# A chunked scan inside a block kernel: the levels' decay factors as products, and one product per head and level

## The reference

```python
f = lbh + (1.0 - lbh) * sig              # forget factor in (0,1), sig = sigmoid(f_pre)
k = (1.0 - lbh) * (1.0 - sig)
# hgrn2_chunk_scan: S_t = diag(f_t) S_{t-1} + k_t v_t^T,   o_t = S_t^T q_t
```

## Time and profile before

| | us |
|---|---|
| median of three runs | 2431.41 (2431.05 to 2433.28) |
| profiled execution | 2433.08 |
| its span | 2431.2 |
| granted clock of TensorE, share of full | 0.992 |
| PE busy | 2378.2 |
| DVE busy | 1647.9 |
| ACT busy | 1178.0 |
| POOL busy | 46.9 |

### The profile page before, as it was taken

One profiled execution on the slowest core, in us unless ns is written; L12 is line 12 of the kernel. 1 busy time (PEld: TensorE's weight loads), 2 busy tenths in 40 slices (PEclk: granted clock), 3 DMA queues, 4 the chain that ended last, 5 costly groups with the idle time before them and its releaser, 6 DMA issues.

```text
span 2431.2 us, 30510 instructions
## 1 busy us (share of the span) xinstructions
PE 2378.2 (98%) x11924; PEld 2020.3 (83%) x11924; DVE 1647.9 (68%) x2155; ACT 1178.0 (48%) x1483; POOL 46.9 (2%) x36
## 2 busy tenths in 40 slices
PE   8999999999999999997999999999999999999998
PEld 8989787888888888886888888887888888888886
DVE  5884756777676676676666777555767567765775
ACT  5443545544544544545555443445655345544554
POOL 0330000000000000000000000000000000000000
PEclk9999999999999999998999999999999999999999
DMA  7434555887888888874988887554555655555554
GB/s 246 139 130 163 175 200 196 296 285 281 285 288 284 274 290 288 276 271 175 338 288 296 285 278 258 185 196 158 189 186 188 194 189 190 186 194 191 186 186 149
DMA packets 152492, 550.06 MB, mean 226 GB/s; under 512 B 17952, under 2 KB 19232, under 8 KB 151456
## 3 DMA queue, kind: packets, MB, share of 16 engines
q1 hardware_dynamic: 152352, 548.12, 66.3%
HBM read 545.94 MB, written 2.11 MB: 225 GB/s over the span
## 4 chain that ended last, share of the span: by engine, by line
PE 92%; DVE 4%; ACT 2%; issue 1%; DMA 1%; SPq 0%; POOL 0%; DVEq 0%; ACTq 0%
PE bank L426 20%; PE bank L428 20%; PE bank L427 20%; PE bank L409 7%; PE mis L409 7%; PE bank L413 3%; PE mis L413 3%; PE bank L397 2%; PE bank L398 2%; PE bank L399 2%; PE mis L427 1%; PE mis L426 1%; PE mis L428 1%; PE mis L518 1%; DVE wlo L1134 1%; PE mis L500 1%
## 5 line engine op out<-in xcount | busy, mean ns | idle before, releaser
L1134 DVE TENSOR_TENSOR wlo<-raw,whi 128x1024 fp32r<-128x1024 f32 x824 | 1005.3, 1225 | 698.9 <-ACT whi L724 698.3
L724 ACT ACTIVATE whi<-raw 128x1024 fp32r<-128x1024 f32 x824 | 868.2, 1059 | 1075.6 <-PE bank L428 650.9
L426 PE MATMUL bank<-whi,xs 128*128 128x512 f32 x1152 | 456.0, 396 | 4.8 <-DVE wlo L1134 3.1
L428 PE MATMUL bank<-wlo,xs 128*128 128x512 f32 x1152 | 450.6, 391 | 0.0
L427 PE MATMUL bank<-whi,xs 128*128 128x512 f32 x1152 | 450.2, 391 | 0.0
L426 PE MATMUL bank<-whi,hs 128*128 128x512 f32 x1072 | 417.9, 390 | 1.3 <-DVE wlo L1134 1.3
L428 PE MATMUL bank<-wlo,hs 128*128 128x512 f32 x1072 | 417.3, 389 | 0.0
L427 PE MATMUL bank<-whi,hs 128*128 128x512 f32 x1072 | 417.2, 389 | 0.0
L426 PEld LDWEIGHTS bank<-whi,xs 128*128 128x128 f32 x1152 | 217.4, 189 | 50.3 <-issue 6.7
L428 PEld LDWEIGHTS bank<-wlo,xs 128*128 128x128 f32 x1152 | 217.3, 189 | 46.1
L427 PEld LDWEIGHTS bank<-whi,xs 128*128 128x128 f32 x1152 | 217.5, 189 | 43.7
(11 more groups left out here) (189 smaller groups left out, 2058.2 us busy)
## 6 DMA issues: line engine op xcount, KB each, us to landing
raw<-wstream SPq DMA_DIRECT2D x824, 512.0 KB, 4.3
aring<-astream SPq DMA_DIRECT2D x192, 512.0 KB, 5.0
x<-xt SPq DMA_DIRECT2D x4, 512.0 KB, 6.6
gvb<-gvrow SPq DMA_DIRECT2D x8, 256.0 KB, 5.6
gate<-gate_rows SPq DMA_DIRECT2D x2, 1024.0 KB, 9.2
out<-acc SPq DMA_DIRECT2D x2, 640.0 KB, 3.6
pw<-poolw SPq DMA_DIRECT2D x1, 1024.0 KB, 10.5
silu_c<-rows SPq DMA_DIRECT2D x1, 1024.0 KB, 5.5
```

Of the source, the lines that this page charges most:

```text
L426: pe.matmul(o, h, whi[:, slot, c], start=first and k == 0, stop=False)
L428: mm = pe.matmul(o, h, wlo[:, slot, c], start=False, stop=last and k == UK - 1)
L724: act.activation(whi[:, slot, :], raw[:, slot, :], ACT.Copy).then_inc(hi_ready, 1)
L1134: dve.tensor_tensor(wlo[:, slot, :], raw[:, slot, :], whi[:, slot, :].bitcast(F32), ALU.subtract).then_inc(lo_ready, 1)
```

## The change

The levels run from small to large (`LEVELS` is now 1, 2, ..., 128) and no logarithm or exponential is taken. An item is the diagonal (`it` = 0) or a level (`it` = 1 to 8); PE does item `it` behind unit `it` + 4 of the half.

- `prep` writes the keys of the second tile of 128 tokens in reversed order. The first query operand is `qq` times the forget factor.
- `grow(hf, it)` on DVE comes ahead of the split at unit `it` + 4. It waits for the products of level `it`, multiplies neighbouring block products of forget factors to those of the next level (`spans`), and multiplies the keys of the left blocks and the queries of the right blocks in place.
- `both(hf, it)` on ACT copies the live half of the keys of each tile into one operand `kc`. Since the second tile is reversed, its left blocks fall where the first tile has right blocks, so both fit in 128 columns.
- `level` then has one product of 128 columns a head: the queries of the right blocks of both tiles, read in place from `qe` with gaps. Half of the result is of no use (keys of one tile with queries of the other), and `keep` takes the rest with two masked copies of 256, one a tile.
- `turn` reverses the second tile's `vv` over its tokens by a product with the reversed unit matrix, so that they fit the reversed rows of `sc`; ACT copies them back. `weigh` moves from behind unit (6,1) to behind (6,3), ACT's copy of its result from (6,3) to (6,5).
- POOL's program goes, and the fills of `kl` and `ones128` at the start. A second mask is loaded, and `eye_back` is made in `bounds`.

```diff
-LEVELS = (128, 64, 32, 16, 8, 4, 2, 1)
+LEVELS = (1, 2, 4, 8, 16, 32, 64, 128)
+ITEMS = 1 + len(LEVELS)
+ITEM_AT = 4
...
+        def item(hf, it):
+            return hf * ITEMS + it
+        def same_bank_before(hf, it):
+            if it >= 3:
+                return item(hf, it - 2)
+            return item(0, ITEMS - 3 + it) if hf else None
+        def span_at(l):
+            return 4 * T - 2 * (4 * T // LEVELS[l])
...
-            def level(hf, l):
-                i = l % 2
-                b = mis[i]
-                pe.wait_ge(h_ops, hf * 8 + l + 1)
-                if two_before(hf, l) is not None:
-                    pe.wait_ge(h_evac, two_before(hf, l) + 1)
-                if LEVELS[l] == 128:
+            def level(hf, it):
+                m, b = LEVELS[it - 1], mis[it % 2]
+                pe.wait_ge(h_ops, hf * len(LEVELS) + it)
+                if same_bank_before(hf, it) is not None:
+                    pe.wait_ge(h_evac, same_bank_before(hf, it) + 1)
+                if m == P:
                     for h in range(4):
-                        mm = pe.matmul(b[:, h * P:(h + 1) * P], kl[:, i, h * T:h * T + P],
-                                       qe[:, i, h * P:(h + 1) * P], start=True, stop=True)
+                        mm = pe.matmul(b[:, h * P:(h + 1) * P], kk[:, h * T:h * T + P], qe[:, h * T + P:(h + 1) * T],
+                                       start=True, stop=True)
                 else:
-                    for s in range(8):
-                        h, tt = s // 2, s % 2
-                        mm = pe.matmul(b[:, s * 64:(s + 1) * 64],
-                                       kl[:, i, h * T + tt * P:h * T + (tt + 1) * P],
-                                       qe[:, i, s * 64:(s + 1) * 64], start=True, stop=True)
+                    pe.wait_ge(h_both, hf * (len(LEVELS) - 1) + it)
+                    for h in range(4):
+                        k = slice(h * P, (h + 1) * P)
+                        mm = pe.matmul(b[:, k].rearrange("p (n m) -> p n m", m=m), kc[:, it % 2, k],
+                                       halves(qe[:, h * T:(h + 1) * T], m)[:, :, 1, :], start=True, stop=True)
                 mm.then_inc(h_sc, 1)
 
             def diagonal(hf):
-                pe.wait_ge(lg_sum, hf + 1)
+                pe.wait_ge(h_keys, hf + 1)
                 if hf:
-                    pe.wait_ge(h_evac, half_level(0, len(LEVELS)) + 1)
+                    pe.wait_ge(h_evac, 1)
                 for s in range(8):
                     h, tt = s // 2, s % 2
                     mm = pe.matmul(mis[2 + tt][:, h * P:(h + 1) * P], kk[:, h * T + tt * P:h * T + (tt + 1) * P],
                                    qq[:, 4 * hf + h, tt * P:(tt + 1) * P], start=True, stop=True)
                 mm.then_inc(h_sc, 1)
 
+            def turn():
+                pe.wait_ge(h_evac, 2 * ITEMS)
+                pe.wait_ge(bank_free, 12)
+                for c in range(2):
+                    mm = pe.matmul(mis[c][:, :], eye_back[:, :], vv[:, 1, c * NC:(c + 1) * NC], start=True, stop=True)
+                mm.then_inc(h_turn, 1)
             def weigh():
-                pe.wait_ge(h_evac, half_level(1, len(LEVELS)) + 1)
-                pe.wait_ge(bank_free, 12)
+                pe.wait_ge(h_turned, 2)
                 for hh in range(HEADS):
                     hf, h = hh // 4, hh % 4
                     c = slice(h * P, (h + 1) * P)
...
-            for l in range(9):
-                work[(2 + (l + 5) // 8, (l + 5) % 8)] = (0, l)
-                work[(4 + (l + 5) // 8, (l + 5) % 8)] = (1, l)
+            for hf, j0 in ((0, 2), (1, 4)):
+                for it in range(ITEMS):
+                    work[(j0 + (it + ITEM_AT) // GU, (it + ITEM_AT) % GU)] = (hf, it)
...
-                        hf, l = work[(j, u)]
-                        level(hf, l) if l < len(LEVELS) else diagonal(hf)
+                        hf, it = work[(j, u)]
+                        level(hf, it) if it else diagonal(hf)
                     if (j, u) == (6, 1):
+                        turn()
+                    if (j, u) == (6, 3):
...
+            def both(hf, it):
+                m = LEVELS[it - 1]
+                act.wait_ge(h_ops, hf * len(LEVELS) + it)
+                if it >= 3:
+                    act.wait_ge(h_sc, item(hf, it - 2) + 1)
+                o = halves(kc[:, it % 2, :], m).rearrange("p (h n) s m -> p h n s m", h=4)
+                k = halves(kk[:, :], m).rearrange("p (h a n) s m -> p h a n s m", h=4, a=2)
+                for a in range(2):
+                    ins = act.activation(o[:, :, :, a, :], k[:, :, a, :, a, :], ACT.Copy)
+                ins.then_inc(h_both, 1)
...
+                    if (j, i) in ((2, 0), (4, 0)):
+                        prep(j // 2 - 1)
...
+                        it = (j - j0) * GU + i - ITEM_AT + 1
+                        if 1 <= it < len(LEVELS):
+                            both(hf, it)
+                    if (j, i) == (6, 1):
+                        act.wait_ge(h_turn, 1)
+                        for c in range(2):
+                            act.activation(vv[:, 1, c * NC:(c + 1) * NC], mis[c][:, :], ACT.Copy).then_inc(h_turned, 1)
+                    if (j, i) == (6, 5):
...
             def prep(hf):
                 dve.wait_ge(h_sg, hf + 1)
...
+                    dve.wait_ge(h_sc, ITEMS)
+                k, g = (a[:, :].rearrange("p (h t) -> p h t", h=4) for a in (kk, sgf))
+                dve.tensor_scalar(k[:, :, 0:P], g[:, :, 0:P], -1.0, 1.0, ALU.mult, ALU.add)
+                link(dve.tensor_scalar(k[:, :, P:T], g[:, :, T - 1:P - 1:-1], -1.0, 1.0, ALU.mult, ALU.add))
+                for h in range(4):
+                    hh, c = 4 * hf + h, slice(h * T, (h + 1) * T)
+                    ins = dve.tensor_scalar(kk[:, c], kk[:, c], oml[:, hh:hh + 1], None, ALU.mult)
+                ins.then_inc(h_keys, 1)
                 for h in range(4):
                     hh, c = 4 * hf + h, slice(h * T, (h + 1) * T)
                     ins = dve.tensor_scalar(fft[:, c], sgf[:, c], oml[:, hh:hh + 1], lbt[:, hh:hh + 1], ALU.mult, ALU.add)
                 ins.then_inc(h_ff, 1)
...
+                dve.wait_ge(h_ff, hf + 1)
...
+                dve.tensor_tensor(qe[:, :], qh, fft[:, :], ALU.mult).then_inc(h_ops, 1)
+            def grow(hf, it):
+                l, m = it - 1, LEVELS[it - 1]
+                n = 4 * T // (2 * m)
+                of = fft[:, :] if l == 0 else spans[:, span_at(l):span_at(l) + 2 * n]
+                of = of.rearrange("p (n s o) -> p n s o", s=2, o=1)
+                dve.wait_ge(h_sc, item(hf, it) + 1)
+                dve.wait_ge(h_ops, hf * len(LEVELS) + it)
+                q = halves(qe[:, :], m)[:, :, 1, :]
+                if m < P // 2:
+                    o = spans[:, span_at(it):span_at(it) + n].rearrange("p (n o) -> p n o", o=1)
+                    dve.tensor_tensor(o, of[:, :, 0, :], of[:, :, 1, :], ALU.mult)
+                f = of.rearrange("p (h a n) s o -> p h a n s o", h=4, a=2)
+                for a in range(2):
+                    k = halves(kk[:, :], m).rearrange("p (h a n) s m -> p h a n s m", h=4, a=2)[:, :, a, :, a, :]
+                    fk = f[:, :, 1, ::-1, 1, :] if a else f[:, :, 0, :, 1, :]
+                    dve.tensor_tensor(k, k, fk.to_broadcast([P, 4, n // 8, m]), ALU.mult)
+                dve.tensor_tensor(q, q, of[:, :, 0, :].to_broadcast([P, n, m]), ALU.mult).then_inc(h_ops, 1)
+            def keep(hf, it):
+                dve.wait_ge(h_sc, item(hf, it) + 1)
+                if it == 0:
...
+                                                  mk[tt][:, NM - P:].rearrange("p (o t) -> p o t", o=1).to_broadcast([P, 4, P]),
...
+                dve.wait_ge(h_evac, item(hf, it))
+                m, b = LEVELS[it - 1], mis[it % 2]
+                if m == P:
...
+                    mask = mk[tt][:, (it - 1) * 64:it * 64].rearrange("p (o n m) -> p o n m", o=1, m=m)
+                    mask = mask.to_broadcast([P, 4, 64 // m, m])
+                    o = sc[:, hf, tt, :, :].rearrange("p h (n s m) -> p h n s m", s=2, m=m)[:, :, :, 1, :]
+                    d = b[:, :].rearrange("p (h s n m) -> p h s n m", h=4, s=2, m=m)[:, :, tt, :, :]
+                    ins = dve.copy_predicated(o, mask, d)
...
+                def before(i, j=j):
+                    for hf, j0 in ((0, 2), (1, 4)):
+                        it = (j - j0) * GU + i - ITEM_AT
+                        if 1 <= it < len(LEVELS):
+                            grow(hf, it)
+                body(j, (lambda j=j: scaled_out(j)) if j in (6, 7) else None, after=after, done=RING if j == 0 else 0,
+                     before=before)
```

126 lines of the change are left out of this document (21 added, 105 removed).

## The result

| | before | after |
|---|---|---|
| median, us (runs of one comparison) | 2432.14 (2431.05 to 2433.28, 4) | 2413.12 (2412.36 to 2414.19, 4) |
| profiled execution | 2433.08 | 2412.84 |
| its span | 2431.2 | 2411.1 |

The ratio is 0.9919, 95% interval 0.9905 to 0.9933. The change brought 19.0 us where 15.1 were forecast; 0.9919 of the 2431.41 that the forecast started from is 2411.7, just under the lower end of the range. The direction was right, and so was the mechanism inside the scan; the size was 3.9 us short, for reasons that lie mostly behind the scan.

The account below looks back on a forecast made before the run. PE, busy 98% of the span, was taken as the bound. 12.2 + 5.5 - 1.8 - 0.8 = 15.1 us saved took the profiled 2433.1 to 2418.0, with the median 1.7 below at 2416.3; range 2413 to 2425.

Parts of the forecast that it names:

- The products, 12.2: On PE in fourteen levels: four products of 128 columns replace eight of 64, 1.75 to 0.88 us a level, 12.2 saved.
- Reading with gaps, nothing: PE's moving operand read from `qe` in runs with gaps: no cost; at worst doubled product time, giving back all 12.2.
- rival C: Reading with gaps doubles the levels' product time, so the 12.2 is not won: 2428.5 us; chance 0.07.
- The waits, 5.5: PE's two long waits for `qe` at each half's first level, and smaller late starts, go: 5.5 us saved.
- `turn`, 1.8: Two added f32 products of 512 columns on PE after unit (6,1), reversing the second tile's values: 1.8 us more.
- The loop, 0.8: From level to level, `grow` on DVE and ACT's key copies slightly overrun one PE unit: 0.8 us lost in all.
- rival D: DVE's multiplies by a repeated factor cost two to three times the plain one: some 2437 to 2454; chance 0.05.
- The second mask, nothing, or under 1 us without its cover: Its 288 KB transfer, queued on SP between units 3 and 4: free since ACT does not wait for unit 4.
- ACT's table loads, nothing: ACT loses eight exponentials and four table loads per pair of halves and gains copies: costed at nothing.
- Behind group 6 all is as before, PE-bound, so a gain made here stays.: After the changed stretch (projection groups 2 to 6) nothing alters the gain: no term added.
- Rival E: Products not fewer in effect, or the gain given back later where something else sets the pace: about 2430; chance 0.06.

Follow-up runs that it names:

- PE's part alone: Kernel before with four products of 128 columns a level in place of eight of 64, second tile's keys left out: 2426.22 us.
- the dummies: Kernel after with 16, 52 and 22 unused f32 products on PE ahead of the three norm waits: 2408.52 us; the same norm dummies were also put in before.
- dummies in its waits: Kernel before with 9 and 12 dummy f32 products in PE's two waits ahead of the first level of each half: 2431.64 us.
- both sets: Kernel before with dummies in its two first-level waits (9 and 12) and ahead of the three norms (16, 52 and 22): 2425.04 us.
- six more and the parameters' transfers moved: Kernel after with the norm dummies, parameters' transfers behind unit 9, and six dummies behind the first norm's three transposes: 2405.85 us.

## Why the forecast was too small, point by point

- **The products, 12.2.** Right. A level went from 1.70 to 1.81 us down to 0.81 to 0.89, which is 12.5 over the 14 levels, and with eight products again 11.4 come back. What stood unsaid is that DVE had to shed its copies as well: PE's part alone brought 5.5.
- **Reading with gaps, nothing.** Right; rival C is out. With runs of one word 0.83, of eight 0.81. Of the two rules of the Trainium skill weighed there, the one on 16-byte lines ("SBUF — State Buffer", The DMA port swizzle) agrees with this, and the one of "Advanced Engine Details and Errata" (Memory Cachelines) does not extend to the operand read from SBUF; the output is written in order here, so no run tests it for PSUM.
- **The waits, 5.5.** Right; both are gone, with the late starts behind them. Against the normal step they add up to 6.0.
- **`turn`, 1.8.** Measured 1.70.
- **The loop, 0.8.** Measured 1.2, within its bounds: levels start 0.25 and 0.54 late in the first half, and 0.34, 0.09 and 0.03 in the second. Its links in the kernel after:

```profile
83.75 0.69 DVE L1254 TENSOR_TENSOR spans<-fft 128x512 f32<-128x512 f32 x1 [1.91 <-PE mis L523]
84.36 0.76 DVE L1259 TENSOR_TENSOR kk<-kk,fft 128x256 f32<-128x256 f32 x2
85.03 0.69 DVE L1260 TENSOR_TENSOR qe<-qe,fft 128x512 f32<-128x512 f32 x1
85.64 1.22 DVE L1131 TENSOR_TENSOR wlo<-raw,whi 128x1024 fp32r<-128x1024 f32 x1
86.77 0.74 DVE L1281 COPY_PREDICATED sc<-mk,mis 128x256 f32<-128x256 int32 x1
87.29 0.81 DVE L1281 COPY_PREDICATED sc<-mk_back,mis 128x256 f32<-128x256 int32 x1
...
94.42 0.43 DVE L1281 COPY_PREDICATED sc<-mk,mis 128x256 f32<-128x256 int32 x1
94.75 0.44 DVE L1281 COPY_PREDICATED sc<-mk_back,mis 128x256 f32<-128x256 int32 x1
```

  `grow` steps 0.61 + 0.67 + 0.61 = 1.89 (forecast 1.94), even with single words and repeated factors, so rival D is out. Section 5.2 of "Vector Engine (DVE) Microarchitecture Reference" in the Trainium skill, by which runs of one word slow the stream, is not borne out here, and the measurement decides. The masked copies at m = 1 and 2 are another matter: 0.52 and 0.59 a step where 0.35 was taken, and 0.33 from m = 4 on. They stand behind the split, and the levels that follow them in the first half (at 90.52 and 94.36) start at the normal step.
- **The second mask, nothing, or under 1 us without its cover.** The cover failed: 0.74 us lost at the start. ACT does not wait for unit 4, but the transfer queued behind unit 3 delays unit 3 itself: its split starts at 21.58 instead of 20.85, and with the mask's transfer moved at 20.79. From 12 to 20 us the transfers already run at 377 to 416 GB/s.
- **ACT's table loads, nothing.** This step failed. The loads in the scan (six before, one after) are hidden, but the last exponential of the scan, at 170.4 us, also decided which table was there when the gates began at 270.9, 100 us on: a load of 1.28 us, for which PE waits. Worth 1.3, shown in the traces from both sides.
- **"Behind group 6 all is as before, PE-bound, so a gain made here stays."** This is the step that failed by most. The work behind is the same, but its granted clock and its waits are not. The first norm took 6.8 us at half clock in the profile of before and 3.4 in that of after, and that alone is 1.7. PE's window over this norm in before:

```profile
385.00:405.00 20.00, 14.96 (x62) 0.83 0.45 170
```

  Each against its own kernel, the dummies win 1.6 at the first norm of before and nothing at that of after, 3.1 and 2.7 behind the start of the second, and 2.6 and 2.4 at the third. So 2.2 us of the distance between the two profiles go away with the half clock.

The 1.1 that the two profiles gain at the second norm (1122.4) is not the clock's. It arises in one wait: from PE's last product to the first transpose pass 13.06 us in before and 12.00 in after.

```profile
1105.98 1.06 ACT L724 ACTIVATE whi<-raw 128x1024 fp32r<-128x1024 f32 x1 [2.99 <-DMA raw<-wstream]
1108.79 2.35 DVE L1134 TENSOR_TENSOR wlo<-raw,whi 128x1024 fp32r<-128x1024 f32 x2
1122.38 1.97 PE L477 MATMUL mis<-eye,xn 128*128 128x128 f32 x8 [12.67 <-DVE xn L1178]
```

and in after:

```profile
1086.43 1.06 ACT L737 ACTIVATE whi<-raw 128x1024 fp32r<-128x1024 f32 x1 [1.47 <-DMA raw<-wstream]
1089.24 2.35 DVE L1131 TENSOR_TENSOR wlo<-raw,whi 128x1024 fp32r<-128x1024 f32 x2
1102.83 1.54 PE L482 MATMUL mis<-eye,xn 128*128 128x128 f32 x6 [11.61 <-DVE xn L1177]
```

DVE empties the last banks only after two splits, and these start 0.53 us ahead of PE's last product in before (1109.32) and 1.59 ahead in after (1090.83), since ACT's split waited longer for its transfer in before. Three executions of before have 13.06 to 13.18 here, and two of after 12.00 and 12.21. Yet the kernel before has 11.75 with dummies in its waits, 11.88 with both sets and 11.99 with four products, and the kernel after has 12.88 with dummies. So, as far as these show, the wait goes with how a kernel's timing meets its transfers, and not with what the change does. It is why the two kernels with dummies are 16.5 apart up to the second norm and 15.5 behind it.

The account up to the gates is: 15.1 forecast, + 0.56 in the scan, + 0.10 for the turn, + 1.30 for the table load, - 0.74 for the mask, which is the 16.3 of the table. Behind the gates the two profiles add 1.7 and 0.5 at the first two norms by the clock, 1.1 by this wait and 0.4 in the MLP, some 20.1 in all. The medians are 19.0 apart. That they are 16.5 apart with the dummies does not make 2.5 the clock's share. The profiles go from 20.1 to 15.4, of which 2.2 are the clock's and 2.1 the wait's, and the medians carry about 1 us of scatter each. Rival E had the gain given back behind the scan; here what lies behind the scan added to it.

Open: why the first norm shows 3.4, 6.8 or 10.2 us at half clock. Kernels that got there 0.8 to 1.2 us earlier than after, or 3.2 later, had more than after, one that got there 2.8 later had the same; before had 6.8 twice and 3.4 once. So one of three executions of before had the short stretch too, and whether after owes it to the change or to luck was not settled. Nor was the 0.4 us that after gains in the MLP against the first profile of before; the last profiled execution of before gains it as well.

## What to carry to other kernels

Halving PE's products pays only if the engine that empties the banks gets lighter with it; try the PE part alone before crediting it. When an activation function goes, look at the next function behind the last one, however far, for its table. Where a kernel bound by PE pauses for 4 to 12 us, price the half clock behind the pause too: resident dummy products brought 4.6 us here, and 7.3 with six more and the parameters' transfers moved, and an edit that only shifts the arrival at the pause can move the time by 1 to 2 us either way.

## What the runs showed of the hardware

- An f32 product of 64 and one of 128 columns cost the same, some 0.21 us, with the moving operand gapped or packed.
- PE's clock fell to half (1.2 for 2.4 GHz) behind idle times of 1.9 and 2.7 us in some executions of one kernel and not in others.
- It also fell at 376 us where PE had been busy 1.52 of 2 us and 0.66 of 2, and not in the kernel that did the same 1.3 us later. Six more products of 0.22 us in the gap kept it up.
- 3.4 us at half clock over transposes that wait for another engine cost nothing; 6.8 us reaching into the products cost 1.6 to 1.7.
- A load of an activation table costs 1.28 us at the first use of the new function, here 100 us behind the last use of the old one, with copies between.
- 288 KB of transfers queued behind a unit of 512 KB that is waited for delayed it by 0.7 us, and all parameters together (1.9 MB) by 4.5 us.
